# Input stage: the last two row blocks are scaled by GpSimd in two steps each instead of by VectorE

## The chip, the cores and the metric

The kernel runs on one core of a Trainium2 chip. Its engines are TensorE (PE, matmuls and transposes; its weight loads are shown as PEld), VectorE (DVE), ScalarE (ACT), GpSimd (POOL) and SyncE (SP, which issues most transfers). Each engine works through its own instructions in order and waits on semaphores for the others. The metric is the device time of one execution in microseconds (us), as the median of several.

## The reference, cut to what matters

The program is one layer of a first model (gated delta rule, dilated attention, MLP) followed by one layer of a second (differential attention, a linear recurrence). The change touches only the first lines: the input `x` (1024 rows of 1024, float32) is normalised row by row and multiplied by a gain row, before the first projection.

```python
def _rmsnorm(x, w):
    xf = x.astype(jnp.float32)
    y = xf * lax.rsqrt(jnp.mean(xf * xf, axis=-1, keepdims=True) + EPS) * w.astype(jnp.float32)
    return y.astype(x.dtype)
...
        h = _rmsnorm(x, ln_mix_pre[l])
        proj = jnp.einsum('bsd,dc->bsc', h, w_in[l]).astype(f32)
```

## The kernel before

The 1024 rows of `x` are eight blocks of 128 rows: `xin[:, i, :]` is block i, one row per partition, 1024 elements along it. SyncE loads them one after the other. Each block then goes through a chain over four engines:

- ScalarE squares the block and sums along the row into a column of `small` (`squares`, L291).
- For two blocks at a time VectorE divides by 1024 and adds epsilon (`eps`, L327), and GpSimd raises the two columns to the power -0.5 (L363).
- VectorE scales the block in place in one instruction, by the column and by the gain row `ln_row` (`normed`, L331).
- TensorE transposes it in eight 128x128 pieces into two PSUM banks (`pe_turn_x`, L372). From block 4 on it first waits until the bank is free again, that is until block i - 3 has been subtracted.
- ScalarE copies each bank, rounded, to the high part of the transposed input (`highs`, L296), and VectorE writes what is left over to the low part (`lows`, L321). A product of two float32 matrices is then done as three matmuls of such parts (`mm3`, L2500 to L2502).

Every `Flow` is a semaphore whose keys are ticked in the order in which they are listed; waiting for a key waits for its place in that list.

The order on each engine is written out by hand. TensorE transposes blocks 0 to 3 alone (`pe_input`). Blocks 4 to 7 are transposed inside the first projection (`pe_prep0` for head 0): its first half (rows 0 to 511) needs blocks 0 to 3 only and consists of eight steps of three matmuls; block 4 is transposed behind step 0, block 5 behind step 2, block 6 behind step 4 and block 7 behind step 6. The second half (rows 512 to 1023) waits at L655 for the subtractions of block 7. VectorE's order is that of `dve_input` (L333 to L355). GpSimd does the four powers (`pool_input`) and next, in `pool_delta`, a few small memsets that wait for the subtractions of block 7 (L1372 to L1376). Everything behind the input stage is the same in both kernels.

Of the kernel before, what the change touches and what calls it, by code (L numbers as in the profile page):

```python
# [6 lines left out]
ALU = mybir.AluOpType  # L7
# [98 lines left out]
def bc(ap, *shape):  # L106
    return ap.to_broadcast(list(shape))
# [13 lines left out]
def program(nc, x, wst, wab, cwt, vecs, gate, relb, meta, lam, lruw, cst, onehot, rope, msk, out):  # L121
    with ExitStack() as ctx:
# [21 lines left out]
        def flow(name, keys, step=1):  # L144
            return Flow(nc, ctx, name, keys, step)

        def A(off, *shape):
            return view(ar[:, off:off + int(np.prod(shape))], shape)

        def R_(off, *shape):  # L150
            return view(wins[off, int(np.prod(shape))][:, :], shape)
# [5 lines left out]
        dve_step, act_step, pool_step = [Chain(nc, ctx, n) for n in ("dve_step", "act_step", "pool_step")]  # L157
# [73 lines left out]
        def dve_ck(v, i):  # L231
            if i < len(CK):
                v.wait_ge(in_hi, i)
                v.do.tensor_tensor(R_(8192 + SLOT * (i % 2), 1024), ck_place(i), R_(9216 + SLOT * (i % 2), 1024).bitcast(F32), ALU.subtract).then_inc(*in_lo.tick(i))
# [9 lines left out]
        small = A(V0 + 168, 88)  # L244
# [6 lines left out]
        xin = A(R + 1024, 8, 1024)  # L251
        junks = [A(R + 9216 + 1024 * i, 1024) for i in range(2)]
        ln_row = A(R + 13184, 1024)
# [4 lines left out]
        first_in = flow("first_in", ["ln", "cst", "vecs"], 16)  # L258
# [4 lines left out]
        norms = ([(n, i) for i in range(8) for n in ("res", "h2")]  # L263
                 + [("m", 0)] + [k for i in range(9) for k in ([("mlp", i)] if i < 8 else []) + ([("u", i - 1)] if i else [])])
        norm_sq = flow("norm_sq", [("x", i) for i in range(8)] + norms + [("y", i, hf) for i in range(8) for hf in range(2)])
        norm_eps = flow("norm_eps", [("x", i) for i in range(4)] + norms)
        norm_pow = flow("norm_pow", [("x", i) for i in range(4)] + norms + [("y", i) for i in range(8)])

        filled = flow("filled", ["half", "raw", "lwt"] + [("lru", i) for i in range(4)] + [(n, i) for i in range(4) for n in ("lru_by", "lru_in")] + ["mask"])
        x_normed = flow("x_normed", range(8))  # L270
        x_turned = flow("x_turned", [(i, hf) for i in range(8) for hf in range(2)])

        dve_const = flow("dve_const", ["conv_w", "masks"])
# [1 line left out]
        def x_bank(i, hf):  # L275

            return bank((2 * i if i < 4 else 2 + 2 * ((i - 4) % 3)) + hf)
# [38 lines left out]
        def dve_input(v):  # L316
            def lows(i):
                for hf in range(2):
                    c = slice(4 * hf, 4 * hf + 4)
                    v.wait_ge(in_hi, (i, hf))  # L320
                    v.do.tensor_tensor(R_(39488, 8, 1024)[:, c, 128 * i:128 * i + 128], x_bank(i, hf).rearrange("p (j n) -> p j n", j=4),  # L321
                                       R_(0, 8, 1024)[:, c, 128 * i:128 * i + 128].bitcast(F32), ALU.subtract).then_inc(*in_lo.tick((i, hf)))

            def eps(k):
                c = slice(2 * k, 2 * k + 2)
                v.wait_ge(norm_sq, ("x", 2 * k + 1))
                v.do.tensor_scalar(small[:, c], small[:, c], 1.0 / 1024, EPS, ALU.mult, ALU.add).then_inc(*norm_eps.tick(("x", k)))  # L327

            def normed(i):
                v.wait_ge(norm_pow, ("x", i // 2))  # L330
                v.do.scalar_tensor_tensor(out=xin[:, i, :], in0=xin[:, i, :], scalar=small[:, i:i + 1], in1=ln_row, op0=ALU.mult, op1=ALU.mult).then_inc(*x_normed.tick(i))  # L331

            eps(0)  # L333
            v.wait_ge(first_in, "vecs")
            normed(0)
            eps(1)
            for i in (1, 2, 3):
                normed(i)
            lows(0)
            lows(1)  # L340
            eps(2)
            lows(2)
            lows(3)
            dve_ck(v, 0)
            normed(4)
            normed(5)
            eps(3)
            lows(4)
            normed(6)
            lows(5)  # L350
            normed(7)
            lows(6)
            lows(7)
            v.wait_ge(const_in, "msk")
            v.do.tensor_scalar(A(V0, 120), A(V0, 120), 0.5, None, ALU.mult).then_inc(*dve_const.tick("conv_w"))  # L355

        def pool_input(p):
            p.do.memset(mh_t, -0.5).then_inc(*filled.tick("half"))
            p.wait_ge(filled, "half")
            for k in range(4):  # L360
                c = slice(2 * k, 2 * k + 2)
                p.wait_ge(norm_eps, ("x", k))
                p.do.tensor_tensor(small[:, c], small[:, c], bc(mh_t, P, 2), ALU.pow).then_inc(*norm_pow.tick(("x", k)))  # L363

        def pe_turn_x(t, i):
            t.wait_ge(x_normed, i)
            for hf in range(2):
                if i >= 4:
                    t.wait_ge(in_lo, (i - 3, hf))
                for j in range(4):  # L370
                    kt = 4 * hf + j
                    o = t.do.transpose(x_bank(i, hf)[:, 128 * j:128 * j + 128], xin[:, i, 128 * kt:128 * kt + 128], ident)  # L372
                o.then_inc(*x_turned.tick((i, hf)))

        def pe_input(t):
            t.wait_ge(first_in, "vecs")
            for i in range(4):
                pe_turn_x(t, i)
# [295 lines left out]
        def pe_prep0(t, h):  # L674
            if h in GATES:
                yield from pe_proj(t, h, "g0")
            for n, _ in enumerate(pe_proj(t, h, "q")):
                if h == 0 and n < 8 and n % 2 == 0:
                    pe_turn_x(t, 4 + n // 2)
                yield  # L680
            for n, _ in enumerate(pe_proj(t, h, "k")):
                if n in (13, 15):
                    pe_flip(t, h, "fq", (n - 13) // 2, chq[h % 2])
                yield
# [3075 lines left out]
        @block.vector  # L3760
        def _(vector):
            v = Engine(vector)
            dve_input(v)
            dve_delta(v)
            stage_ends(v, "dve", 1)
            dve_dilated(v)
            stage_ends(v, "dve", 2)
            dve_branches(v)
            stage_ends(v, "dve", 3)
            dve_rows(v)  # L3770
            dve_ff(v)
            dve_lru(v)
            stage_ends(v, "dve", 6)
            dve_rope(v)
            stage_ends(v, "dve", 7)
            dve_values(v)
            stage_ends(v, "dve", 8)
            dve_diff(v)

        @block.gpsimd  # L3780
        def _(gpsimd):
            p = Engine(gpsimd)
            pool_input(p)
            pool_delta(p)
            stage_ends(p, "pool", 1)
            stage_ends(p, "pool", 2)
            pool_branches(p)
            stage_ends(p, "pool", 3)
            pool_rows(p)
            pool_ff(p)  # L3790
            pool_lru(p)
            stage_ends(p, "pool", 6)
            pool_mask(p)
            stage_ends(p, "pool", 7)
            stage_ends(p, "pool", 8)
            pool_diff(p)
# [157 lines left out]
```

## Time and profile before

| | us |
|---|---|
| median of 3 runs | 3101.1 |
| lowest, highest | 3099.65, 3101.7 |
| profiled execution | 3101.83 |
| its span | 3099.9 |
| TensorE busy | 3013.0 |
| VectorE busy | 1558.6 |
| ScalarE busy | 1072.9 |
| GpSimd busy | 366.3 |

The profile is of one execution; its times count from the start of the span. A row of the timeline gives the start, the duration, the engine, the line of the kernel, the operation, the tensors written and read with their shapes, and in brackets how long the engine had been idle before and what ended that. Consecutive instructions of one kind are put together as xN. `ar` is the large SBUF array that holds nearly all float32 data, `r` a rounded view of it, `ps` is PSUM.

### The profile page before, as it was taken

The numbers are of one execution on the slowest core, as the hardware profiler recorded it, in microseconds if no ns is written. First come the engines' busy times: TensorE is split into PE (matmuls) and PEld (weight loads), VectorE is DVE, ScalarE is ACT, GpSimd is POOL, SyncE is SP. The second block draws the span as 40 slices with busy tenths as digits, with TensorE's granted clock in tenths as the row PEclk, the third lists the DMA queues.
The fourth block names the chain that finished last, engine by engine and source line by source line (L and its number), as shares of the span: only waits on it lengthen the run. The fifth ranks groups of instructions, "written<-read, shape, count | busy, mean of one in ns | idle before, by whom it ended". The sixth has DMA issues, their size and how long they took to land.

```text
span 3099.9 us, 39140 instructions
## 1 busy us (share of the span) xinstructions
PE 3013.0 (97%) x16315; PEld 2530.8 (82%) x16315; DVE 1558.6 (50%) x2184; ACT 1072.9 (35%) x2306; POOL 366.3 (12%) x433
## 2 busy tenths in 40 slices
PE   7999999999999999999999999999999999999998
PEld 5788888888888877877878888888888888888887
DVE  5566666667653224032147545444454488643453
ACT  4443453454442213232332341112111244314453
POOL 0122232232231000000000000000000022001111
PEclk9999999999999999999999999999999999998999
DMA  3211111111112111111263321111111141102001
GB/s 120 69 51 52 42 55 48 35 42 35 35 45 65 41 58 52 45 42 55 101 226 110 124 100 61 41 55 41 55 54 42 62 140 41 55 28 76 28 28 42
DMA packets 59649, 193.37 MB, mean 62 GB/s; under 512 B 7728, under 2 KB 15536, under 8 KB 50256
## 3 DMA queue, kind: packets, MB, share of 16 engines
q1 hardware_dynamic: 58464, 189.26, 17.7%
q8 instruction: 129, 2.11, 0.3%
q10 hardware_dynamic: 1008, 1.61, 0.2%
q14 instruction: 48, 0.39, 0.0%
HBM read 156.86 MB, written 33.98 MB: 62 GB/s over the span
## 4 chain that ended last, share of the span: by engine, by line
PE 87%; DVE 7%; ACT 3%; issue 1%; DMA 1%; POOL 0%; SPq 0%; ACTq 0%; POOLq 0%; DVEq 0%
PE ps L2500 22%; PE ps L2502 22%; PE ps L2501 21%; PE ps L728 3%; PE ps L734 3%; PE ps L1729 2%; PE ps L3382 1%; PE ps L3445 1%; PE ps L740 1%; PE ps L771 1%; PE ps L765 1%; PE ps L1694 1%; PE ps L759 1%; PE ps L711 1%; PE ps L780 1%
## 5 line engine op out<-in xcount | busy, mean ns | idle before, releaser
L2500 PE MATMUL ps<-r,r 128*128 128x512 f32 (+3 forms) x2992 | 1172.6, 392 | 24.9 <-DVE ar L3630 4.4
L2502 PE MATMUL ps<-r,r 128*128 128x512 f32 (+3 forms) x2992 | 1114.0, 372 | 0.0
L2501 PE MATMUL ps<-r,r 128*128 128x512 f32 (+3 forms) x2992 | 1112.0, 372 | 0.0
L2500 PEld LDWEIGHTS ps<-r,r 128*128 128x128 f32 x2992 | 564.7, 189 | 118.5 <-issue 19.7
L2502 PEld LDWEIGHTS ps<-r,r 128*128 128x128 f32 x2992 | 562.9, 188 | 99.9
L2501 PEld LDWEIGHTS ps<-r,r 128*128 128x128 f32 x2992 | 565.2, 189 | 81.1 <-issue 2.5
L2500 PE MATMUL ps<-r 128*128 128x512 f32 x512 | 199.7, 390 | 0.8 <-DVE r L2489 0.8
L2502 PE MATMUL ps<-r 128*128 128x512 f32 x512 | 199.2, 389 | 0.0
L2501 PE MATMUL ps<-r 128*128 128x512 f32 x512 | 199.2, 389 | 0.0
L2761 DVE TENSOR_TENSOR ar<-ar,ps 128x512 f32<-128x512 f32 x224 | 150.8, 685 | 89.7 <-PE ps L2502 89.6
L2484 ACT ACTIVATE r<-ar 128x2048 fp32r<-128x2048 f32 x48 | 91.7, 1910 | 268.1 <-PE ps L2502 252.3
L1237 DVE COPY_PREDICATED ar<-mk,ar 128x512 f32<-128x512 uint8 x80 | 79.5, 994 | 135.2 <-ACT ar L1029 134.9
L2489 DVE TENSOR_TENSOR r<-ar,r 128x2048 fp32r<-128x2048 f32 x48 | 109.8, 2288 | 55.5 <-ACT r L2484 55.5
L1623 DVE TENSOR_TENSOR r<-ar,r 128x2048 fp32r<-128x2048 f32 (+1 forms) x24 | 50.9, 2120 | 168.5 <-ACT r L1618 168.5
L2708 DVE TENSOR_TENSOR ar<-ar 128x512 f32<-128x512 f32 x64 | 44.3, 691 | 173.7 <-ACT ar L2640 173.7
L1357 POOL TENSOR_SCALAR ar<-ar 128x128 f32<-128x128 f32 x128 | 100.8, 799 | 205.3 <-PE ps L771 205.3
L1137 DVE SCALAR_TENSOR_TENSOR ar<-ar 128x1024 f32<-128x1024 f32 x96 | 123.1, 1282 | 1.6
L728 PEld LDWEIGHTS ps<-ar 128*128 128x128 f32 x768 | 96.9, 191 | 29.1 <-DVE ar L1241 15.4
L1024 ACT ACTIVATE ar<-ps 128x512 f32<-128x512 f32 x96 | 57.4, 598 | 178.4 <-PE ps L728 178.4
L728 PE MATMUL ps<-ar 128*128 128x128 f32 x768 | 106.5, 281 | 11.2 <-DVE ar L1241 6.5
L2500 PEld LDWEIGHTS ps<-r 128*128 128x128 f32 x512 | 96.1, 188 | 21.0 <-DVE r L2489 1.2
L2502 PEld LDWEIGHTS ps<-r 128*128 128x128 f32 x512 | 96.1, 188 | 20.0
(325 smaller groups left out, 3968.8 us busy)
## 6 DMA issues: line engine op xcount, KB each, us to landing
ar<-wst SPq DMA_DIRECT2D x72, 1024.0 KB, 4.8
ar<-wst SPq DMA_DIRECT2D x56, 512.0 KB, 3.9
ar<-x SPq DMA_DIRECT2D x16, 512.0 KB, 5.7
ar<-sc_g SPq DMA_DIRECT2D x32, 256.0 KB, 4.6
sc_h<-ar SPq DMA_DIRECT2D x32, 256.0 KB, 2.1
sc_x<-ar SPq DMA_DIRECT2D x16, 512.0 KB, 2.7
ar<-sc_x SPq DMA_DIRECT2D x16, 512.0 KB, 4.3
sc_b<-ar SPq DMA_DIRECT2D x24, 260.0 KB, 2.0
```

Source lines behind the costliest of these rows:

```text
L728: o = t.do.matmul(q4(bank(4), j), q4(MT, j), mixed(FB0, b, j), start=True, stop=True)
L734: o = t.do.matmul(q4(bank(3), j), q4(Yb, j), mixed(BT, b, j), start=True, stop=True)
L1137: o = v.do.scalar_tensor_tensor(out=tmp, in0=r_[:, j:j + 1024], scalar=w[:, j:j + 1], in1=tmp, op0=ALU.mult, op1=ALU.add)
L1237: v.do.copy_predicated(mixed(BT, b), blocked(mk[:, n, :], b), blocked(Xb if n < 6 else bank(3), b)).then_inc(*inv_dve.tick(k(("XT", n))))
L1357: o = p.do.tensor_scalar(q4(kd[g % 2], d), q4(sqk[q], c), db[q][d][:, POS[c]:POS[c] + 1], None, ALU.mult)
L1729: o = t.do.matmul(q4(bank(6), hh), PT3[0:m, 2 * hh + j, :], Vt[g][0:m, ci, 128 * hh:128 * hh + 128], start=(j == 0), stop=(j == len(parts) ...
L2484: a.do.activation(w_set(j)[0], place, ACT.Copy).then_inc(*w_hi.tick(j))
L2489: v.do.tensor_tensor(lo, w_slot(W2 + j)[0], hi.bitcast(F32), ALU.subtract).then_inc(*w_lo.tick(j))
L2500: t.do.matmul(o, l[0], r[0], start=first, stop=False)
L2501: t.do.matmul(o, l[0], r[1], start=False, stop=False)
L2502: return t.do.matmul(o, l[1], r[0], start=False, stop=last)
L2761: v.do.tensor_tensor(dst, dst, bk, ALU.add).then_inc(*ff2_acc.tick(k))
```

## The change

VectorE scales blocks 0 to 5 only. Blocks 6 and 7 are scaled by GpSimd behind its last power, in two instructions each: a multiplication by the block's column (`tensor_scalar`), and, after a wait for it, one by the gain row (`tensor_tensor`). Their completion is counted in `norm_pow` instead of `x_normed`, and TensorE waits for them there. On VectorE the epsilon step of blocks 6 and 7 (`eps(3)`) moves ahead of the scaling of block 5, and the four pairs of subtractions of blocks 4 to 7 follow one another.

```diff
-        norm_pow = flow("norm_pow", [("x", i) for i in range(4)] + norms + [("y", i) for i in range(8)])
+        norm_pow = flow("norm_pow", [("x", i) for i in range(4)] + [("normed", i) for i in (6, 7)] + norms + [("y", i) for i in range(8)])
...
-        x_normed = flow("x_normed", range(8))
+        x_normed = flow("x_normed", range(6))
...
             normed(4)
+            eps(3)
             normed(5)
-            eps(3)
-            lows(4)
-            normed(6)
-            lows(5)
-            normed(7)
-            lows(6)
-            lows(7)
+            for i in range(4, 8):
+                lows(i)
...
                 p.do.tensor_tensor(small[:, c], small[:, c], bc(mh_t, P, 2), ALU.pow).then_inc(*norm_pow.tick(("x", k)))
+            p.wait_ge(first_in, "vecs")
+            p.wait_ge(norm_pow, ("x", 3))
+            for i in (6, 7):
+                p.do.tensor_scalar(xin[:, i, :], xin[:, i, :], small[:, i:i + 1], None, ALU.mult).then_inc(*pool_step.tick())
+                p.wait_ge(pool_step, pool_step.n)
+                p.do.tensor_tensor(xin[:, i, :], xin[:, i, :], ln_row, ALU.mult).then_inc(*norm_pow.tick(("normed", i)))
 
         def pe_turn_x(t, i):
-            t.wait_ge(x_normed, i)
+            t.wait_ge(x_normed if i < 6 else norm_pow, i if i < 6 else ("normed", i))
```

## Rows read from the trace of the kernel before

**Rows 1.** Page, part 1: busy time, share of the span and instructions of each engine.
```profile
PE 3013.0 (97%) x16315; PEld 2530.8 (82%) x16315; DVE 1558.6 (50%) x2184; ACT 1072.9 (35%) x2306; POOL 366.3 (12%) x433
```

**Rows 2.** Chain of waits, 23 to 37 us: start, us, what.
```profile
23.30 0.79 PE ps L2500
...
33.53 0.45 PE ps L372 x4
...
34.00 0.61 ACT r L296
...
34.63 1.30 DVE r L321 x2
```

**Rows 3.** Timeline of TensorE, 0 to 70 us.
```profile
12.36 6.82 PE L372 MATMUL ps<-ar 128*128 128x128 f32 x32 [12.36 <-DVE ar L331]
...
31.11 1.04 PE L372 MATMUL ps<-ar 128*128 128x128 f32 x8
...
33.37 1.04 PE L372 MATMUL ps<-ar 128*128 128x128 f32 x8
...
35.98 0.50 PE L2500 MATMUL ps<-r,r 128*128 128x512 f32 x1 [0.88 <-DVE r L321]
```

**Rows 4.** Timeline of VectorE, 0 to 70 us.
```profile
10.92 1.29 DVE L331 SCALAR_TENSOR_TENSOR ar<-ar 128x1024 f32<-128x1024 f32 x1 [0.96 <-POOL ar L363]
12.82 0.17 DVE L327 TENSOR_SCALAR ar<-ar 128x2 f32<-128x2 f32 x1 [0.61 <-ACT ar L291]
12.90 1.28 DVE L331 SCALAR_TENSOR_TENSOR ar<-ar 128x1024 f32<-128x1024 f32 x1
...
19.64 2.48 DVE L321 TENSOR_TENSOR r<-ps,r 128x512 fp32r<-128x512 f32 x4
...
23.16 2.47 DVE L331 SCALAR_TENSOR_TENSOR ar<-ar 128x1024 f32<-128x1024 f32 x2
...
27.93 1.27 DVE L331 SCALAR_TENSOR_TENSOR ar<-ar 128x1024 f32<-128x1024 f32 x1
...
31.33 1.28 DVE L331 SCALAR_TENSOR_TENSOR ar<-ar 128x1024 f32<-128x1024 f32 x1
...
34.63 1.29 DVE L321 TENSOR_TENSOR r<-ps,r 128x512 fp32r<-128x512 f32 x2 [0.83 <-ACT r L296]
```

**Rows 5.** Timeline of ScalarE, 0 to 80 us.
```profile
23.66 0.22 ACT L291 ACTIVATION_READ_ACCUMULATOR ar<-ar 128x1 f32 x1
```

**Rows 6.** Timeline of GpSimd, 0 to 100 us.
```profile
13.07 1.67 POOL L363 TENSOR_TENSOR ar<-ar 128x2 f32<-128x2 f32 x1 [2.26 <-DVE ar L327]
19.81 0.69 POOL L363 TENSOR_TENSOR ar<-ar 128x2 f32<-128x2 f32 x1 [5.06 <-DVE ar L327]
25.80 0.69 POOL L363 TENSOR_TENSOR ar<-ar 128x2 f32<-128x2 f32 x1 [5.29 <-DVE ar L327]
```

**Rows 7.** Instructions of single GpSimd lines: shortest/median/longest ns, first and last start.
```profile
L1357 POOL TENSOR_SCALAR ar<-ar x128: 595/606/2634, 158.3 to 1008.9; 128x128 f32<-128x128 f32 x128
...
L3695 POOL TENSOR_SCALAR ar<-ar x32: 374/374/723, 2844.8 to 3078.8; 128x128 f32<-128x128 f32 x32
...
L3144 POOL TENSOR_TENSOR ar<-ar x4: 2397/2630/2780, 2560.2 to 2642.9; 128x1040 f32<-128x1040 f32 x4
...
L3683 POOL TENSOR_SCALAR ar<-ar x8: 192/192/193, 2896.6 to 3094.7; 128x1 f32<-128x1 f32 x8
...
L3129 POOL MEMSET ar<- x1: 964/964/964, 2528.8 to 2528.8; 128x1024 f32 x1
```

**Rows 8.** Timeline of GpSimd, 2840 to 2870 us: two steps, the second waiting.
```profile
2850.46 0.19 POOL L3690 TENSOR_SCALAR ar<-ar 128x1 f32<-128x1 f32 x1 [1.00 <-ACT ar L3526]
2850.73 0.55 POOL L3692 TENSOR_TENSOR ar<-ar 128x1 f32<-128x1 f32 x1
```

**Rows 9.** Timeline of TensorE, 80 to 93 us.
```profile
90.05 0.74 PE L2500 MATMUL ps<-r,r 128*128 128x512 f32 x1 [1.92 <-ACT ps L878]
```

**Rows 10.** Windows: stretch, length, busy PE, PEld, DVE, ACT, POOL, PEclk, DMA, GB/s.
```profile
90.07:93.49 3.42, 3.42 (x7) 2.25 (x8) 3.14 (x7) 0.38 (x2) 2.65 (x1) 0.50 0.41 110
```

## The prediction

> **What bounds the kernel now.** I read the page's busy shares first: TensorE is at work 97% of the span and GpSimd 12% [rows 1], so an instruction moved between VectorE and GpSimd counts only where TensorE waits for it. Then the chain of waits through the stage that is changed [rows 2]: from 23.30 us on the chain is TensorE's own matmuls and transposes, one behind the other, up to the last transposes of block 7, then a ScalarE copy, two VectorE subtractions and TensorE again at 35.98. So there are two places where the normalised blocks 6 and 7 can matter. The first is TensorE's order: transposes of block 6 at 31.11 and of block 7 at 33.37, each behind the matmuls that stand before it in the program; neither row shows idle time, so both blocks were ready when their turn came [rows 3]. The second is the tail behind block 7: TensorE idles 0.88 us before 35.98 for VectorE's subtractions, and VectorE itself had idled 0.83 us before these, for ScalarE [rows 3, 4].
>
> The VectorE rows show how early the blocks were: the scaling of block 7 began at 31.33 and took 1.28, so it ended at 32.61, 0.76 before its transposes [rows 4]. That of block 6, the same instruction at 27.93, ended at 29.21, 1.90 before.
>
> **What is removed.** Two scalings of 1.28 us leave VectorE. This shortens nothing on the path: the last subtractions, those of block 7, were released by ScalarE and not by VectorE's queue, as its 0.83 us of idle time says [rows 4], and ScalarE's copy comes out of the transposes. Those before them (blocks 5 and 6) are awaited only by matmuls behind 35.98, and block 4's by the transposes of block 7, several microseconds after they are done. Removed: 0 us of the end, with TensorE's own queue as the cover; I see no gain even as a bound, because between 23.30 and the end of block 7's transposes the chain holds no step of VectorE [rows 2].
>
> **What is moved: the last power.** The mean's epsilon for blocks 6 and 7 goes ahead of the scaling of block 5. It needs ScalarE's sum of squares, read out at 23.66 + 0.22 = 23.88 [rows 5], so it starts when the scaling of block 4 ends: the pair of scalings takes 23.16 to 25.64, the second of 1.28, so at about 24.35. Block 5's scaling follows 0.08 later, as at 12.82 and 12.90 [rows 4], and runs from 24.43 to 25.71. GpSimd's power of 128x2 would start at about 24.6 and run 0.69, but the row at 13.07 shows what it does beside such a scaling: 1.67 instead of 0.69, ended at 14.74, which is 0.56 behind the scaling's end at 14.18 [rows 4, 6]. I therefore end it at 25.71 + 0.56 = 26.27, against 26.49 before [rows 6]. Moving it brings 0.2 us, not the 1.2 that its place in the program suggests, and block 5 is later by 0.08 with three microseconds to spare before its transposes.
>
> **What is added.** GpSimd does, for each of two blocks, a 128x1024 multiplication by a column, a wait for itself, and a 128x1024 multiplication by the gain row; all four stand in one queue, and the transposes wait for the second and the fourth. Behind them in GpSimd's queue are only the small memsets that waited for the subtractions of block 7 anyway.
>
> The second multiplication has a close row: 128x1040, two full operands, 2397 ns at least and 2630 in the median [rows 7]; I take 2.40. Nothing beside it should lengthen it: VectorE then does only subtractions that read PSUM and one SBUF tile, and the power at 19.81, beside four of them, took 0.69, as the one at 25.80 did with VectorE idle [rows 4, 6]. If they did collide, the same line's later instances of up to 2.78 would add 0.4 per step.
>
> The first multiplication has no row of its size, and is the term on which the sum hangs. The same form (one operation with a column) at 128x128 takes 606 ns in the median; a form with two operations, also with a column, takes 374 at that size; two-operation forms of 128x1 take 192 [rows 7]. Lower bound: a 128x1024 memset, 0.96 us, which reads nothing [rows 7]. By the two-operation form, (374 - 192) / 127 = 1.43 ns an element, hence 0.19 + 1023 x 1.43 ns = 1.66. By the one-operation form with the same 192 as its fixed part, 3.26 ns an element, hence 3.53. Upper bound, eight times 606: 4.85. The rows don't say whether the 232 ns between the two forms are a fixed price or one for each element. I take 606 for the first 128 elements and 1.43 ns for each of the other 896, 1.88 us: the fixed price, as one operation less should not cost more than twice as much on every element.
>
> Here a row and a rule of the Trainium skill differ. The row is the 606 ns above: a memset eight times as wide took 964 [rows 7]. The page "GPSIMD Engine Reference", section "4.1 Engine selection", says that a one-input operation runs on GpSimd at roughly line rate and a two-input one about half as fast as on VectorE. By that rule the sum would be that of the first rival below; by the row it is more.
>
> **The sum.** Dependent GpSimd steps follow each other after about 0.08 (2850.46 + 0.19 to 2850.73) [rows 8]; I use 0.09. To TensorE I count 0.15, as from the end of the first scaling (10.92 + 1.29) to the first transposes at 12.36 [rows 3, 4].
> Block 6: 26.36 + 1.88 = 28.24; + 0.09 + 2.40 = 30.73; transposes possible at 30.88, before their turn at 31.11. No loss.
> Block 7: starts at once, 30.73 + 1.88 = 32.61; + 0.09 + 2.40 = 35.10; transposes at 35.25 instead of 33.37. TensorE stands still 1.88 us, and everything behind comes that much later: the tail has no slack, as the transposes of block 7 set ScalarE, VectorE and the first matmul of the next half.
> The profiled execution took 3101.83 with a span of 3099.9; with 1.88 its time would be 3103.7. It lies 0.7 above the median of the runs, 3101.1; from the median the forecast is **3103 us**, 0.06% more.
>
> One cost is left open, TensorE's granted clock. Later in the trace an idle stretch of 1.92 us [rows 9] was followed by 3.42 us at 0.50, the lower of its two levels, 1.2 instead of 2.4 GHz [rows 10]: that costs 3.42 x 0.5 = 1.7 us. The new pause, together with the 0.88 behind it, could bring the same. I leave it out of the forecast's value and take it into its range, 3102 to 3105.
>
> **The rivals.**
> First, hidden: the column multiplication goes at the memset's pace, 0.96. Then block 6 is done at 26.36 + 0.96 + 0.09 + 2.40 = 29.81 and block 7, another 3.45 behind it, at 33.26; its transposes start at 33.41, 0.04 late. Time unchanged, 3101. For it speaks the memset; against it both column forms, whose 374 and 606 ns at 128 elements leave little of 0.96 for the other 896.
> Second, the other side: the one-operation form costs 3.26 ns on every element, 3.53 us. Block 6 is then done at 29.89 + 2.49 = 32.38 and transposed 1.4 late (32.53); block 7 at 32.38 + 3.53 + 2.49 = 38.40, transposed at 38.55, 5.18 late. TensorE idles 1.4 and 3.8 us close together, more than the pause that halved the clock, so 1.7 comes on top: 3101.1 + 6.9 = 3108. It parts from the forecast at 2.1 us for the column multiplication, from where block 6 comes late too (26.36 + 2.1 + 2.49 + 0.15 = 31.1), and crosses 0.2% (6.2 us, about what a measurement of this kernel can tell from no change) only with the slower clock. For it: the same form in this very kernel, with a steady 595 to 606. At 4.85 a step block 7 is done at 26.36 + 2 x (4.85 + 0.09 + 2.40) = 41.04 and 7.8 late; with the 1.7 that is 3110.6.
> Third, faster: the freed VectorE would let the second half of the first projection begin before 35.98. The subtractions of block 7 would have to come earlier, and they hang on TensorE's own queue through ScalarE. The most that is in it is the 0.2 us of the power, 3100.9, and that is spent on the way.
>
> **How the numbers follow.** Forecast 0.50 (all within 0.2%), hidden 0.16 (within), slow column form 0.31 (of it 0.24 beyond 0.2%, 0.07 within, where the clock holds), faster 0.03. Hence faster 0.03, no change 0.73, slower 0.24. The range goes from the hidden case, less the 1.4 by which a run of before lay under their median (3099.65), to above the second rival with its clock: 3099.7 to 3109.
>
> **What would show it.** In the changed kernel GpSimd's four new rows give the two durations directly: about 1.9 and 2.4, with the power ending near 26.3. The transposes of block 6 should start at 31.1 with no idle time, those of block 7 near 35.25 after some 1.9 us of idle time put down to GpSimd, and the matmul that began at 35.98 at about 37.9. VectorE's subtractions of blocks 5 and 6 should come no later. The forecast is wrong if the column multiplication lasts over 2.1 us, if VectorE's subtractions lengthen the GpSimd steps, if the power ends near 25.3 (then there is no block by the scaling), or if the granted clock falls behind the pause.

## The result, and the profile after

The changed kernel took 3107.88 us in the median of 12 runs (3104.93 to 3110.57), the kernel before 3101.52 in 12 runs of the same comparison (3099.65 to 3106.11). The ratio is 1.0020, with a 95% interval of 1.0011 to 1.0028: slower by 0.2%, 3.4 to 8.7 us. The forecast of 3103 was too low by 5; the range held. The profiled execution took 3107.63, with a span of 3105.8.

The chain of waits of the changed kernel through the stage (start, us, what) no longer runs through TensorE's queue [rows 2], but through GpSimd's:

```profile
24.50 1.68 POOL ar L359
...
26.35 2.86 POOL ar L363
...
29.29 2.37 POOL ar L365
31.66 2.84 POOL ar L363
...
34.57 2.35 POOL ar L365
...
36.97 0.67 PE ps L374 x4
...
37.66 0.61 ACT r L296
...
38.29 1.30 DVE r L321 x2
...
39.63 0.79 PE ps L2502
```

GpSimd's timeline (start, us, engine, line, operation, operands) has the power beside VectorE's scaling and the four new steps:

```profile
24.50 1.67 POOL L359 TENSOR_TENSOR ar<-ar 128x2 f32<-128x2 f32 x1 [4.09 <-DVE ar L327]
26.35 2.85 POOL L363 TENSOR_SCALAR ar<-ar 128x1024 f32<-128x1024 f32 x1 [0.19 <-POOL ar L359]
29.29 2.37 POOL L365 TENSOR_TENSOR ar<-ar 128x1024 f32<-128x1024 f32 x1
31.65 2.84 POOL L363 TENSOR_SCALAR ar<-ar 128x1024 f32<-128x1024 f32 x1
34.57 2.34 POOL L365 TENSOR_TENSOR ar<-ar 128x1024 f32<-128x1024 f32 x1
```

TensorE's timeline has what follows, against [rows 3]: 1.00 us of idle time ahead of block 6 and 2.77 ahead of block 7, both put down to GpSimd, where there was none:

```profile
31.71 1.09 PE L374 MATMUL ps<-ar 128*128 128x128 f32 x8 [1.00 <-POOL ar L365]
...
36.97 1.22 PE L374 MATMUL ps<-ar 128*128 128x128 f32 x8 [2.77 <-POOL ar L365]
...
39.63 0.79 PE L2502 MATMUL ps<-r,r 128*128 128x512 f32 x1 [0.17 <-DVE r L321]
```

The second half began at 39.63 instead of 35.98, 3.65 us later. The rest is the granted clock. The windows of the changed kernel (stretch, length, busy PE, PEld, DVE, ACT, POOL, then the clock's share, DMA share and GB/s) show it at half behind block 7's pause and once more at 96 us:

```profile
37.83:41.24 3.41, 3.24 (x10) 2.13 (x8) 1.42 (x3) 2.37 (x4) 0.19 (x4) 0.50 0.03 7
...
95.86:99.27 3.41, 3.41 (x7) 1.89 (x7) 3.07 (x9) 0.49 (x1) 1.64 (x1) 0.50 0.10 26
99.27:102.68 3.41, 3.41 (x8) 1.92 (x7) 0.26 (x1) 0.00 (x0) 0.00 (x0) 0.50 0.48 119
```

Both programs issue the same 16315 matmuls in the same order, so the n-th of one trace can be set against the n-th of the other (where a kernel below adds transposes, these are left out). By that the distance to before was 3.65 us where the second half begins, 4.37 from 40 to 88 us, 5.9 from 102 us on and 5.8 at the end. So 3.65 are the wait, 0.7 the half clock behind it, and 1.5 arose at 96 us, where before had the lower clock for 3.4 us [rows 10] and this execution for 6.8.

### The profile page after: what moved, and what is told of

The parts are those of the page before. It is cut to its first block, busy times and chain, and to the rows that moved or that the text cites. A ratio compares the mean times of both kernels' runs of the same rounds, so it can differ in the third digit from the quotient of the medians.

```text
span 3105.8 us, 39143 instructions
## 1 busy us (share of the span) xinstructions
PE 3015.5 (97%) x16315; PEld 2531.5 (82%) x16315; DVE 1556.0 (50%) x2182; ACT 1072.9 (35%) x2306; POOL 377.7 (12%) x437
## 4 chain that ended last, share of the span: by engine, by line
PE 86%; DVE 7%; ACT 3%; issue 1%; DMA 1%; POOL 1%; SPq 0%; ACTq 0%; POOLq 0%; DVEq 0%
PE ps L2502 22%; PE ps L2504 21%; PE ps L2503 21%; PE ps L730 3%; PE ps L736 3%; PE ps L1731 2%; PE ps L3384 1%; PE ps L3447 1%; PE ps L742 1%; PE ps L773 1%; PE ps L767 1%; PE ps L1696 1%; PE ps L761 1%; PE ps L713 1%; PE ps L782 1%
```

## The experiments

Each was timed against the kernel before in alternating runs (7 to 12 runs of the kernel and 12 to 33 of before in a comparison), but for the one in pieces, which ran once. I put the distance of matmuls to the profiled execution of before beside the medians, because it places a microsecond that the totals can't: runs of one kernel are several microseconds apart.

| kernel | block 7 transposed | second half begins | distance at 85 us | at 135 us | median; before there | ratio, 95% |
|---|---|---|---|---|---|---|
| before | 33.37 | 35.98 | | | | |
| the change | 36.97 | 39.63 | 4.4 | 5.9 | 3107.88; 3101.52 | 1.0011 to 1.0028 |
| only block 7 | 33.16 | 35.77 | -0.2 | -0.2 | 3100.58; 3102.09 | 0.9990 to 1.0008 |
| two operations | 33.61 | 36.28 | 0.3 | 1.8 | 3103.61; 3102.09 | 0.9993 to 1.0010 |
| order only | 32.54 | 35.15 | -0.8 | -1.8 | 3100.65; 3102.09 | 0.9989 to 1.0006 |
| waits filled | 36.98 | 39.65 | 3.7 | 5.1 | 3107.26; 3102.09 | 1.0006 to 1.0024 |
| in pieces | 38.00 | 41.38 | 6.7 | 6.5 | 3110.30 (one execution) | |
| one step more | 39.92 | 43.30 | 7.7 | 9.2 | 3111.91; 3100.48 | 1.0023 to 1.0045 |
| weights on GpSimd | 32.48 | 35.09 | -0.9 | -0.9 | 3100.94; 3100.48 | 0.9990 to 1.0008 |
| late only | 36.31 | 38.93 | 2.9 | 1.6 | 3105.16; 3101.35 | 0.9999 to 1.0018 |
| the change again | 37.06 | 39.73 | 3.8 | 3.0 | 3108.53; 3101.35 | 1.0011 to 1.0032 |

**Block 7 alone on GpSimd.** VectorE keeps block 6, between the subtractions of blocks 4 and 5.

```diff
-            for i in (6, 7):
+            for i in (7,):
                 p.do.tensor_scalar(xin[:, i, :], xin[:, i, :], small[:, i:i + 1], None, ALU.mult).then_inc(*pool_step.tick())
```

> Part of the change alone: GpSimd scales block 7 only, VectorE keeps block 6 (between the subtractions of blocks 4 and 5). Theory (the loss is GpSimd's chain of four steps arriving late at the transposes of block 7): one block's two steps, 2.85 + 0.08 + 2.37 us behind the power's end at 26.2, are done by 31.7, or by about 33 if VectorE's scaling of block 6 holds them up; the transposes of block 7 come at 33 to 33.4 with at most 0.3 us of idle time, and the time is that of before within 1 us, 3101.5. Beside that, VectorE's scaling of block 6 is released near 27.9, while GpSimd's first step runs: if the two engines exclude each other there, it ends only near 30.5 instead of 29.2. Rival (any large elementwise step on GpSimd slows the stage, by contention or by its wait): at least half of the loss stays, 3104 or more.

The loss is gone, and TensorE has no idle time ahead of either block; block 7's transposes:

```profile
33.16 1.04 PE L376 MATMUL ps<-ar 128*128 128x128 f32 x8
```

One block's steps end at 31.61, 1.5 us before the turn at 33.16. So GpSimd's work costs nothing as long as it is done by then. The side expectation failed: VectorE's scaling of block 6 was not held up. The timelines of GpSimd, and then of VectorE, show both at their usual length side by side:

```profile
26.27 2.86 POOL L365 TENSOR_SCALAR ar<-ar 128x1024 f32<-128x1024 f32 x1 [0.19 <-POOL ar L361]
29.21 2.40 POOL L367 TENSOR_TENSOR ar<-ar 128x1024 f32<-128x1024 f32 x1
```
```profile
27.75 1.27 DVE L331 SCALAR_TENSOR_TENSOR ar<-ar 128x1024 f32<-128x1024 f32 x1
```

**The column multiplication with two operations.**

```diff
-                p.do.tensor_scalar(xin[:, i, :], xin[:, i, :], small[:, i:i + 1], None, ALU.mult).then_inc(*pool_step.tick())
+                p.do.tensor_scalar(xin[:, i, :], xin[:, i, :], small[:, i:i + 1], 1.0, ALU.mult, ALU.mult).then_inc(*pool_step.tick())
```

> The change, with GpSimd's column multiplication given a second operation, a multiplication by 1.0 (the form that took 374 ns at 128x128 in the trace of before, against 606 for the one-operation form). Theory (the one-operation form is the slower one for each element): 0.19 + 1023 x 1.43 ns = 1.66 us instead of 2.85; block 6 is ready in time, block 7 is transposed near 34.6 instead of 36.97, so 1.2 us behind before, and the time is 3102.5 to 3104. Rival (the difference at 128 elements is a fixed price, or comes from the place of the data): 2.6 to 2.85 us, transposes of block 7 near 36.5 to 37, time as with the change, 3107.

An operation more made the instruction two and a half times as fast, faster than even the theory had it. GpSimd's timeline:

```profile
26.41 1.12 POOL L363 TENSOR_SCALAR ar<-ar 128x1024 f32<-128x1024 f32 x1 [0.19 <-POOL ar L359]
27.61 2.38 POOL L365 TENSOR_TENSOR ar<-ar 128x1024 f32<-128x1024 f32 x1
29.97 1.12 POOL L363 TENSOR_SCALAR ar<-ar 128x1024 f32<-128x1024 f32 x1
31.18 2.38 POOL L365 TENSOR_TENSOR ar<-ar 128x1024 f32<-128x1024 f32 x1
```

From the 374 ns at 128 elements [rows 7] that is (1123 - 374) / 896 = 0.84 ns an element, against (2848 - 606) / 896 = 2.50 for the one-operation form; each slope rests on one line at 128 elements and another at 1024. Block 7 still comes 1.08 us late (TensorE's idle time before 33.61): TensorE's own queue would have reached it at 32.5 in this execution, earlier than the 33.37 of before, since the clock rose earlier (the next experiment has more on this). The time can't be told from that of before.

**The moved step alone.**

```diff
             normed(4)
+            eps(3)
             normed(5)
-            eps(3)
```

> Only the moved step: the epsilon of blocks 6 and 7 ahead of the scaling of block 5, VectorE scales all eight blocks. Theory: the power takes 1.67 us beside the scaling and ends near 26.2, no transpose moves, the time is that of before, 3101.5 within 1 us. Rival (the order costs, since block 5 is scaled later): the transposes of block 5 come later than 28.3 to 28.6, and some of the loss is here.

The power again took 1.66 us from 24.51, and the moved step changed nothing else. The transposes of blocks 5 to 7 came 0.8 us earlier than in before, for another reason: the granted clock was at 0.50 from 23.8 to 27.2 here, 3.4 us instead of the 6.8 of before. The same shorter stretch is in the executions with two operations, filled waits, pieces, one step more and late only; those of before, of the change, of block 7 alone, of the weights and of the change again had the longer one. It goes by execution and not by kernel: late only does the same as before up to there, and pieces, one step more and filled waits the same as the change, yet these four have the shorter stretch, and before and the change the longer. It is worth 0.8 us.

**The waits filled.** TensorE repeats transposes of block 5 into banks not yet in use while it would wait.

```diff
+            if i >= 6:
+                t.wait_ge(in_lo, (i - 3, 1))
+                for n in range(8 if i == 6 else 24):
+                    t.do.transpose(x_bank(i, 0)[:, 0:128], xin[:, 5, 0:128], ident)
             t.wait_ge(x_normed if i < 6 else norm_pow, i if i < 6 else ("normed", i))
```

> The change, with 8 and 24 transposes of block 5 repeated into the still unused banks of blocks 6 and 7, ahead of TensorE's wait for them: the same waits for GpSimd, but TensorE isn't idle in them. Theory (of the 6 us about 3.65 are the wait for GpSimd, and the rest is the granted clock, which falls to 0.50 behind the pauses): block 7 is again transposed near 37, with the granted clock at 1.00 then and in the microseconds behind; the first matmul of the second half comes near 39.5 and the following ones 0.23 us apart instead of 0.43; the time is some 1 to 2.5 us lower than that of the change, 3105 to 3106.5. Rival (the pause has no part in it, the rest arises elsewhere): time as with the change, 3107.9.

The clock stayed up in the stretch where it had fallen, block 7 came at 36.98, as with the change, and the distance at 85 us is 3.65 instead of 4.37. The same window as above, in this kernel:

```profile
37.83:41.24 3.41, 2.54 (x13) 1.80 (x12) 1.42 (x3) 2.29 (x4) 0.19 (x4) 1.00 0.01 2
...
95.86:99.27 3.41, 3.41 (x7) 1.95 (x8) 2.65 (x8) 0.49 (x1) 0.92 (x1) 0.50 0.06 13
```

So of the loss in the change's profiled execution 0.7 us was the half clock behind the pause. The expected 1 to 2.5 in the total didn't come (0.6 by the medians, within their scatter): the stretch at 96 us was there again, with TensorE idle for only 0.15 us ahead of block 7, so the pause there doesn't make it. It stands behind another idle stretch, the 1.92 us of [rows 9], which all eleven profiled executions have at the same place of the program: in four the clock was at 0.50 for 6.8 us behind it, in three for 3.4, and in four not at all.

**In pieces.**

```diff
+                for c in range(0, 1024, 512 if i == 6 else 256):
+                    d = slice(c, c + (512 if i == 6 else 256))
+                    p.do.tensor_scalar(xin[:, i, d], xin[:, i, d], small[:, i:i + 1], None, ALU.mult).then_inc(*pool_step.tick())
```

> The change, with GpSimd's one-operation column multiplication cut into pieces: two of 512 for block 6, four of 256 for block 7. The same form took 606 ns at 128 elements and 2850 at 1024. Theory (a fixed part and a price for each element, (2850 - 606) / 896 = 2.50 ns, so 0.29 us fixed): 1.57 us a piece of 512 and 0.93 a piece of 256, 3.1 and 3.7 us for the blocks, block 7 transposed near 38.1 instead of 36.97. Rival (the price goes by elements alone): 1.42 and 0.71 us, 2.85 for either block, transposes of block 7 unmoved at 37.

The law holds. GpSimd took 1.57 us for 512 elements and 0.92 for 256, and block 7 was transposed at 38.00, where 38.1 was expected:

```profile
26.36 3.12 POOL L365 TENSOR_SCALAR ar<-ar 128x512 f32<-128x512 f32 x2 [0.19 <-POOL ar L359]
29.57 2.36 POOL L367 TENSOR_TENSOR ar<-ar 128x1024 f32<-128x1024 f32 x1
31.90 3.62 POOL L365 TENSOR_SCALAR ar<-ar 128x256 f32<-128x256 f32 x4
```

**One step more.**

```diff
+                if i == 7:
+                    p.do.tensor_scalar(xin[:, i, :], xin[:, i, :], mh_t, None, ALU.mult).then_inc(*pool_step.tick())
+                    p.wait_ge(pool_step, pool_step.n)
```

> The change, with a second one-operation column multiplication of block 7 on GpSimd (by the constant column -0.5, so the values of block 7 are other ones): one more step of the suspected cost, 2.85 + 0.08 us. Theory (everything behind the transposes of block 7 hangs on them, microsecond for microsecond): block 7 is transposed near 39.9, the second half begins near 42.6, and the time is 2 to 4 us above that of the change, 3110 to 3112. Rival (part of a delay is taken up later): the distance to before at 400 us into the program is less than 6 us, and the time less than 3109.

Block 7 was transposed 2.95 us later than with the change:

```profile
39.92 1.97 PE L377 MATMUL ps<-ar 128*128 128x128 f32 x8 [5.70 <-POOL ar L368]
```

The second half began at 43.30 rather than 42.6 because the clock was at half there, and the distance to before stood at 9.2 from 380 us to 1035 us. Nothing up to there takes the delay up.

**Late only.** The kernel before, with 34 repeated transposes ahead of those of block 7 and no new work on GpSimd.

```diff
             t.wait_ge(x_normed, i)
+            if i == 7:
+                t.wait_ge(in_lo, (4, 1))
+                for n in range(34):
+                    t.do.transpose(x_bank(i, 0)[:, 0:128], xin[:, 5, 0:128], ident)
```

> The kernel before, without any new work on GpSimd, but with 34 transposes of block 5 repeated into the unused bank ahead of those of block 7: TensorE itself makes block 7 some 3.7 us late. Theory (the lateness of block 7's transposes is the whole loss in the input stage, and GpSimd's steps cost nothing beside it): every matmul from the second half on comes 3.5 to 4 us later than in before, up to 85 us, and the time is that of the change with its waits filled, 3105 to 3107.5. Rival (GpSimd's steps hurt in another way too, by VectorE's or the transfers' slowing down): the time is clearly lower than 3105.

TensorE's timeline has the filling, block 7 and the first matmul of the second half:

```profile
32.60 3.87 PE L370 MATMUL ps<-ar 128*128 128x128 f32 x34
36.31 1.04 PE L376 MATMUL ps<-ar 128*128 128x128 f32 x8
...
38.93 0.50 PE L2504 MATMUL ps<-r,r 128*128 128x512 f32 x1 [0.87 <-DVE r L321]
```

The filling took 3.71 us of the queue (32.60 to 36.31), and the second half began 2.95 later than in before, that is 3.78 later than in the order-only execution with the same early clock. The median is 3.8 above before's. So in the trace lateness alone costs what it lasts; of the totals, the ratio's interval reaches 0.9999. The change's medians lie about 3 us above this one's. That is no sign of another cost of GpSimd's steps: among runs with the same granted clock the two are level, as the last item of the account of the prediction shows.

**The change again.**

> The change once more, for another profiled execution. In the first one the distance to before was 4.4 us at 85 us and 5.9 from 102 us on, since the granted clock was at 0.50 for 6.8 us there and for 3.4 in before. Theory (where such a stretch falls, and how long it is, differs from execution to execution and isn't set by the change): the four GpSimd steps and the transposes come at the same times within 0.2 us, the distance at 85 us is 3.5 to 5 us, and that behind 102 us may be anything from 2 to 6. Rival (the change itself lengthens the stretch at 96 us): again 6.8 us at 0.50 there.

The steps came at the same times (block 7 at 37.06). This execution had the lower clock neither behind the pause nor at 96 us; the window that was at 0.50 before:

```profile
37.83:41.24 3.41, 2.54 (x13) 1.81 (x12) 1.42 (x3) 2.29 (x4) 0.19 (x4) 1.00 0.03 7
95.86:99.27 3.41, 3.41 (x13) 1.91 (x11) 2.76 (x8) 0.49 (x1) 1.03 (x1) 1.00 0.06 13
```

Its distance to before is 3.76 at 85 us and 3.0 from 117 us on, and its time 3105.21, near the lowest of the change. So the wait, 3.65 and 3.75, is there in both executions; the half clock behind it only in one.

**Another step for GpSimd.** VectorE scales all blocks as before; GpSimd makes the low part of the first weights, and ScalarE its high part earlier (the renaming of semaphore keys is left out).

```diff
             highs(0)
+            a.wait_ge(in_loaded[0], 0)
+            a.do.activation(R_(9216, 1024), ck_place(0), ACT.Copy).then_inc(*norm_sq.tick("ck0"))
             highs(1)
...
-            dve_ck(v, 0)
             normed(4)
...
+                if k == 2:
+                    p.wait_ge(norm_sq, "ck0")
+                    p.wait_ge(x_normed, 3)
+                    p.do.tensor_tensor(R_(8192, 1024), ck_place(0), R_(9216, 1024).bitcast(F32), ALU.subtract).then_inc(*filled.tick("ck0"))
```

> The kernel before (VectorE scales all blocks), with another step given to GpSimd: the low part of the first weight block, a subtraction of 128x1024 that VectorE did right before TensorE's first matmul. ScalarE makes its high part earlier (between its copies of blocks 0 and 1), and GpSimd subtracts beside VectorE's subtractions of blocks 0 to 3, from 17.1 to 19.5 us. Theory (an engine's relief counts only where its queue is on the chain, as VectorE's is from 14.7 to 23.2 us): TensorE's first matmul comes at 22.0 to 22.2 instead of 23.2, block 7 is transposed 1.1 us earlier than in before at the same clock, and the time is 1 us lower, 3100 to 3101.5, which the comparison of totals can't separate from before. Rival (GpSimd and VectorE hold each other up, or ScalarE's earlier step delays its copies): the first matmul at 23 us or later, time as before or above.

GpSimd's subtraction ran beside VectorE's, whose first four still took 2.48 us, and TensorE's first matmul came 1 us earlier, at 22.31 where 22.0 to 22.2 was expected, since it still waited for VectorE's subtractions (GpSimd's timeline, then TensorE's):

```profile
17.39 2.37 POOL L364 TENSOR_TENSOR r<-ar,r 128x1024 fp32r<-128x1024 f32 x1 [2.66 <-DVE ar L332]
19.86 0.69 POOL L367 TENSOR_TENSOR ar<-ar 128x2 f32<-128x2 f32 x1
```
```profile
22.31 0.77 PE L2504 MATMUL ps<-r,r 128*128 128x512 f32 x1 [3.52 <-DVE r L322]
```

With the lower clock lasting as long as in before (21.0 to 27.9), the distance was -0.9 from there to 1035 us. The totals can't confirm a gain of 0.03%: 0.9999, 0.9990 to 1.0008.

## Why the prediction was right or wrong

- **Bound and cover: right.** The place was the one named, TensorE's own queue up to block 7, and relieving VectorE brought nothing: with block 7 alone on GpSimd, where the steps are in time, the stage is that of before.
- **The moved power: right.** 24.50 to 26.17, forecast 24.6 to 26.27. It is lengthened beside VectorE's scaling: 1.67 us here, 0.70 in the weights execution, where no scaling ran beside it.
- **The second multiplication: right**, 2.34 to 2.40 for 2.40.
- **The column multiplication: the term that failed.** I took 1.88 us; it was 2.85, beyond the 2.1 that I had named as the point where the forecast ends. The step at fault was "the fixed price, as one operation less should not cost more than twice as much on every element". It costs three times as much on every element: 2.50 ns against 0.84. The fixed parts that these slopes leave, 0.29 and 0.27 us, hardly differ; for the one-operation form the sizes of 256 and 512 fit as well, for the other there are the two sizes alone. The slope of 1.43 for the two-operation form was wrong too, since I had taken its fixed part from 128x1 instructions of 192 ns; two sizes of one form are needed, and the trace of before had only one of each. The row called "a steady 595 to 606" goes up to 2634 [rows 7]; none of the new steps was lengthened so. By the Trainium skill's "GPSIMD Engine Reference", section "4.1 Engine selection", a one-input operation goes at roughly line rate. If the memset's pace (0.96 us for 1024 [rows 7]) is taken for that rate, as in the first rival, the two-operation form comes near it with 1.12, and the one-operation form of this kernel, with 2.85, doesn't.
- **The sum.** With 2.85 the same working gives 26.35 + 2 x (2.85 + 0.08 + 2.37) = 36.95 for the end of block 7's steps; its transposes came at 36.97. Block 6 was late too, where the sum had no loss: TensorE idled 1.00 us ahead of it in one execution and 0.52 in the other. The wait is 3.65 to 3.75 us instead of 1.88.
- **The clock, left open.** It fell behind the pause in one of two profiled executions of the change, and cost 0.7 us there, not 1.7: half of the stretch lay in the tail behind block 7, where TensorE's slower matmuls only filled time in which it waits anyway (0.17 us idle before 39.63 instead of 0.88 [rows 3]). The two other executions with TensorE idle ahead of block 7 for as long or longer, in pieces and one step more, had it at 0.50 for 6.8 us, from 37.3 on, at a cost of 2.1 and 1.1 us: the distance to before grows from 4.63 and 6.55 at block 7 to 6.69 and 7.68 at 45 us.
- **The case.** I had given 0.73 to a change of no more than 0.2%; the measured one is just beyond it. Its 3107.88 lies at the second rival's 3108, but that agreement is luck, as it came by other parts: the rival had 5.2 us of wait and 1.7 of clock. Shown are 3.7 and up to 0.7. Medians of two comparisons are 6.4 and 7.2 above before, and both intervals (3.4 to 8.7, 3.4 to 9.9 us) hold the 3.7 to 4.4.
- **The rest of the time.** The other 2 to 3 us go with the mean granted clock of each run, which is on record. Among the runs at 0.990 the median is 3105.19 for the change (6 of 20 runs), 3105.70 for late only (6 of 11) and 3102.11 for before (31 of the 71 whose clock is on record). So at the same clock the change is some 3 us above before and level with late only; the clock is on record to 0.001, and within a kernel 0.001 less goes with some 2 us more (before: 3100.09 at 0.991, 3102.11 at 0.990). The change's 20 runs had 0.9888 in the mean, late only's 0.9905 and before's 0.9901. Why the change's were lower stays open: the stretch behind block 7's pause is one place for it, the one at 96 us comes and goes in other kernels as well, and filled waits, without the pause, had 0.9895.

## What to carry to other kernels

Work that leaves a busy engine gains only if that engine's queue is on the chain where it leaves; here VectorE's was up to 23 us and no longer behind, so a relief of 1.2 us was worth 0.9 in the one place and one of 2.6 nothing in the other. What the receiving engine may take is the time from its last input to the turn of the one that waits: one block's two steps fitted into it, two blocks' four steps did not. For an instruction not in the trace at its size, take two sizes of the same form before trusting a slope, and try a neighbouring form: on GpSimd the column multiplication with a second, idle operation took 1.12 us instead of 2.85.

## What the runs showed of the hardware that was not expected

- GpSimd's `tensor_scalar` with one operation took 606, 924, 1568 and 2848 ns at 128, 256, 512 and 1024 elements; with two operations 374 at 128 and 1123 at 1024.
- VectorE's scaling with two SBUF tensors took its usual 1.27 us beside GpSimd's one-operation column multiplication (2.86), though such a scaling stretches GpSimd's power of 128x2 from 0.69 to 1.67 us. In the first case, seen in one execution, GpSimd had started earlier; in the second, seen in every trace, VectorE. The order alone doesn't explain it. In the trace of before, VectorE's instruction of the same form at L1143, 1.22 us in the median, took 1.99 when it began 0.13 us into a GpSimd `tensor_tensor` and ended 1.08 behind it:

```profile
208.15 1.04 POOL L1327 TENSOR_TENSOR ar<-ar 128x512 f32<-128x512 f32 x1 [2.05 <-ACT ar L1002]
208.28 1.99 DVE L1143 SCALAR_TENSOR_TENSOR ar<-ar 128x1024 f32<-128x1024 f32 x1
```

So what GpSimd is doing matters too; which of its instructions hold VectorE up was not tested.

- Where the granted clock is low differs between executions of one kernel: of the change's two, one had it at 0.50 behind block 7's pause and for 6.8 us at 96 us, the other at neither place. Around 25 us into the program it was at 0.50 for 3.4 us in some executions and 6.8 in others, worth 0.8 us of the whole, and behind one and the same idle stretch of 1.92 us for 6.8, 3.4 or 0 us.
